# A gating unit that begins on an input whose norm is still being computed

## The reference, cut to what matters

```python
def rms_norm(x, g):
    y = x * lax.rsqrt(jnp.mean(x * x, axis=-1, keepdims=True) + EPS)
    return y * g

def adaln_input(h, mod, j, g):
    return rms_norm(h, g) * (1 + mod[:, :, 3 * j + 1]) + mod[:, :, 3 * j]

def sgu_mixer(xn, w_in, v_g, w_s, b_s, w_out):      # w_in: 1024 x 4096, w_out: 2048 x 1024
    u, v = jnp.split(jax.nn.gelu(xn @ w_in, approximate=False), 2, axis=-1)
    v = rms_norm(v, v_g)
    vg = v.reshape(B, nc, SGU_CHUNK, SGU_GROUPS, gw)          # chunks of 128 positions, 8 groups of 256
    sv = jnp.einsum('gts,bcsgd->bctgd', w_s, vg) + b_s.T[None, None, :, :, None]
    gated = u.reshape(B, nc, SGU_CHUNK, SGU_GROUPS, gw) * sv
    return gated.reshape(B, S, SGU_WIDTH) @ w_out

hp = hp + adaln_gate(m_ctx, 1) * sgu_mixer(adaln_input(hp, m_ctx, 1, norm_g[i, 1]), ...)
```

## Time and profile before

| | |
|---|---|
| median of 3 runs | 1591.44 us (1590.52 to 1593.1) |
| profiled execution, time | 1590.23 us |
| its span, first to last instruction | 1588.4 us |
| mean granted clock of PE | 0.989 |
| PE busy | 1541.1 us, 97% |
| DVE busy | 1106.8 us, 70% |
| ACT busy | 588.1 us, 37% |
| POOL busy | 71.5 us, 5% |
| down projection in front of the gating unit ends | 1078.0 us |
| gating unit's output projection begins | 1237.7 us |

### The profile page before, as it was taken

One profiled execution on the slowest core, in us unless ns is written; L12 is line 12 of the kernel. 1 busy time (PEld: TensorE's weight loads), 2 busy tenths in 40 slices (PEclk: granted clock), 3 DMA queues, 4 the chain that ended last, 5 costly groups with the idle time before them and its releaser, 6 DMA issues.

```text
span 1588.4 us, 23570 instructions
## 1 busy us (share of the span) xinstructions
PE 1541.1 (97%) x9183; PEld 1511.4 (95%) x9183; DVE 1106.8 (70%) x1501; ACT 588.1 (37%) x814; POOL 71.5 (5%) x55
## 2 busy tenths in 40 slices
PE   6999999989989999999999999998999999999999
PEld 6899999989749999999999999998999999999999
DVE  6868787867887877878878788776654355454423
ACT  3333332254474433332343333226434244333321
POOL 2000000023100100000020000001000010000000
PEclk9999999989999999999999999998999999999999
DMA  9255555635223354565635545563623432333332
GB/s 384 96 215 208 188 198 199 239 114 186 81 70 135 122 207 174 177 232 212 225 111 204 189 165 204 214 236 111 234 81 132 152 113 106 117 122 132 119 119 93
DMA packets 49648, 262.72 MB, mean 165 GB/s; under 512 B 6704, under 2 KB 7984, under 8 KB 27568
## 3 DMA queue, kind: packets, MB, share of 16 engines
q1 hardware_dynamic: 49584, 261.82, 45.2%
HBM read 259.57 MB, written 2.23 MB: 165 GB/s over the span
## 4 chain that ended last, share of the span: by engine, by line
PE 87%; DVE 5%; issue 3%; ACT 2%; DMA 2%; SPq 1%; POOL 1%; DVEq 0%; ACTq 0%; POOLq 0%
PE ps L1132 25%; PE ps L1131 25%; PE ps L1133 25%; PE ps L1165 3%; PE ps L1166 2%; PE ps L1168 2%; DVE mprod L746 1%; DMA raw_x<-panels 1%; ACT w_hi L506 1%; PE ps L1351 1%; PE ps L1434 1%; DVE x_lo L809 1%; DVE w_lo L738 1%; DMA raw<-panels 1%; PE ps L1211 0%
## 5 line engine op out<-in xcount | busy, mean ns | idle before, releaser
L506 ACT ACTIVATE w_hi<-raw 128x2048 fp32r<-128x2048 f32 x165 | 316.2, 1917 | 662.3 <-PE ps L1133 521.8
L1131 PE MATMUL ps<-x_hi,w_hi 128*128 128x386 f32 (+1 forms) x1536 | 524.4, 341 | 12.7 <-DVE x_lo L809 8.5
L738 DVE TENSOR_TENSOR w_lo<-raw,w_hi 128x2048 fp32r<-128x2048 f32 x163 | 373.2, 2290 | 233.0 <-ACT w_hi L506 231.9
L1132 PE MATMUL ps<-x_lo,w_hi 128*128 128x386 f32 (+1 forms) x1536 | 523.2, 341 | 0.0
L1133 PE MATMUL ps<-x_hi,w_lo 128*128 128x386 f32 (+1 forms) x1536 | 521.8, 340 | 0.0
L746 DVE SCALAR_TENSOR_TENSOR mprod<-mraw,cB 128x1024 f32<-128x1024 f32 x256 | 313.1, 1223 | 7.4
L1131 PEld LDWEIGHTS ps<-x_hi,w_hi 128*128 128x128 f32 x1536 | 290.6, 189 | 15.9 <-issue 6.7
L1132 PEld LDWEIGHTS ps<-x_lo,w_hi 128*128 128x128 f32 x1536 | 291.5, 190 | 0.5
L1133 PEld LDWEIGHTS ps<-x_hi,w_lo 128*128 128x128 f32 x1536 | 290.7, 189 | 0.0
L1133 PE MATMUL ps<-act_hi,w_lo 128*128 (+1 forms) x832 | 279.6, 336 | 0.0
L1131 PE MATMUL ps<-act_hi,w_hi 128*128 (+1 forms) x832 | 279.6, 336 | 0.0
(11 more groups left out here) (142 smaller groups left out, 1107.7 us busy)
## 6 DMA issues: line engine op xcount, KB each, us to landing
raw<-panels SPq DMA_DIRECT2D x165, 1024.0 KB, 5.0
mraw<-mod_rows SPq DMA_DIRECT2D x128, 512.0 KB, 3.5
mshift<-mod_rows SPq DMA_DIRECT2D x8, 512.0 KB, 15.8
raw_x<-panels SPq DMA_DIRECT2D x4, 1024.0 KB, 5.3
mscale<-mod_scale SPq DMA_DIRECT2D x6, 512.0 KB, 12.5
bias<-na_bias SPq DMA_DIRECT2D x1, 2048.0 KB, 8.2
h<-x_in_t SPq DMA_DIRECT2D x1, 1536.0 KB, 11.2
out<-h SPq DMA_DIRECT2D x4, 384.0 KB, 2.6
```

The source lines that it names most:

```text
L506: nc.scalar.activation(w_hi[q0 % 2][:, :], raw[q0 % 2][:, :], ACT.Copy).then_inc(hi_done, 1)
L738: nc.vector.tensor_tensor(w_lo[q0 % 2][:, :], raw[q0 % 2][:, :], w_hi[q0 % 2][:, :].bitcast(F32), ALU.subtract).then_inc(lo_done, 1)
L1131: mm(out, w[0][:, cols], xs[0], start=start, stop=False)
L1132: mm(out, w[0][:, cols], xs[1], start=False, stop=False)
```

## The change

The gating unit now begins with first_pair, like an FFN: panel G (U0, number Q_G = 109) and the spare panel (U1) on h * scale, then U2 (Q_U2 = 110) on the same x. While PE works on U2, ACT and DVE replace x in place, chunk by chunk, by the plain input that V needs, using four slots of sq. V0 follows, alone and chunk by chunk, then V1 to V7, U3, the mixing, and U4 to U7. The three early U panels are evicted with the factor to a new tile u_early and get their Gelu between V1 and V3. Their product with svb, rounding and subtraction are placed behind those of U3, U4 and U5 (U_TURNS). There is one more spare panel, loaded during the down projection before, and the panels behind it are numbered one lower.

```diff
+Q_G, Q_U2, Q_V, Q_U, Q_OUT1 = 109, 110, 111, 116, 124
+EARLY = (0, 1, 2)
+U_TURNS = (3, 0, 4, 1, 5, 2, 6, 7)
 # SP
+            def gate_behind_down():
+                sp.wait_ge(pe_done, down_panel(2))
+                spare_panel(3)
-            down(down_panel(2), GU, MOD_AT[2] + MOD_GU, MOD_DN[2])
+            down(down_panel(2), GU, MOD_AT[2] + MOD_GU, MOD_DN[2], gate_behind_down)
+            panel(Q_G, 0)
+            panel(Q_U2, 0)
...
-            for g in range(8):
+            for g in range(len(EARLY), 8):
                 panel(Q_U + g, 0)
 # POOL
-            norm(4, 4)
+            norm(4)
 # ACT
-            down(down_panel(2), GU)
-            squares(4)
+            down(down_panel(2), GU, lambda: split_spare(3))
+            scale_h(4, (NMOD + 3) * KD, 3)
+            split(Q_U2, 0)
+            split(Q_V, 0)
+            for k in range(KD):
+                base = (NMOD + 3) * KD
+                act.wait_ge(xv_scaled, k + 1)
+                for cond, cols in ((0, CTX), (1, LAT)):
+                    last = nc.scalar.activation(sq[:, k % 4, cols], sq[:, k % 4, cols], ACT.Identity,
+                                                bias=modT[:, base + k, cond:cond + 1], scale=aT[:, k, cond:cond + 1])
+                last.then_inc(xv_shifted, 1)
+                act.wait_ge(xv_shifted, k + 1)
+                if k < KD - 1:
+                    act.wait_ge(u2_done, k + 1)
+                else:
+                    act.wait_ge(pe_done, Q_U2 + 1)
+                nc.scalar.activation(x_hi[:, k, 0:T], sq[:, k % 4, :], ACT.Copy).then_inc(xvh_done, 1)
             split(Q_V + 1, 0)
-            make_x(4, (1, 1))
+            def early_gelu(g):
+                act.wait_ge(u_scaled, g + 1)
+                for a in range(2 * g, 2 * g + 2):
+                    for cond, cols in ((0, CTX), (1, LAT)):
+                        last = nc.scalar.activation(u_early[:, a, cols], u_early[:, a, cols], ACT.Gelu,
+                                                    bias=u_early[:, a, T + cond:T + cond + 1])
+                last.then_inc(silu_done, 1)
...
+                if 1 <= g <= len(EARLY):
+                    early_gelu(EARLY[g - 1])
-            for g in range(8):
-                done = UPAIR + g
-                act.wait_ge(pe_done, Q_U + g + 1)
-                act.wait_ge(actl_done, done)
-                bk = 2 * (g % 2)
-                nc.scalar.activation(tmp[:, 0:2, 0:T], ps[:, bk:bk + 2, 0:T], ACT.Gelu).then_inc(silu_done, 1)
-                split(Q_U + g + 2, 0)
+            for turn, g in enumerate(U_TURNS):
+                done = UPAIR + turn
+                at = 2 if g in EARLY else 0
+                if g not in EARLY:
+                    act.wait_ge(pe_done, Q_U + g + 1)
+                    act.wait_ge(actl_done, UPAIR + (U_TURNS.index(g - 1) + 1 if g - 1 not in EARLY else 0))
+                    bk = u_bank(g)
+                    nc.scalar.activation(tmp[:, 0:2, 0:T], ps[:, bk:bk + 2, 0:T], ACT.Gelu).then_inc(silu_done, 1)
+                    split(Q_U + g + 2, 0)
                 act.wait_ge(mul_done, done + 1)
-                nc.scalar.activation(act_hi[:, 2 * g:2 * g + 2, :], tmp[:, 0:2, 0:T], ACT.Copy).then_inc(acth_done, 1)
+                nc.scalar.activation(act_hi[:, 2 * g:2 * g + 2, :], tmp[:, at:at + 2, 0:T], ACT.Copy).then_inc(acth_done, 1)
 # DVE
-            down(down_panel(2), GU, 3, (1, 0), 0.5, MOD_AT[2] + MOD_GU, MOD_DN[2])
-            rms(4, Q_V + 1)
-            make_x(4)
+            down(down_panel(2), GU, 3, (1, 0), 0.5, MOD_AT[2] + MOD_GU, MOD_DN[2], spare=3)
+            split(Q_U2, 0)
+            factor(4)
+            def scale_t(k):
+                if k >= 4:
+                    dve.wait_ge(xv_done, k - 3)
+                nc.vector.tensor_tensor(sq[:, k % 4, :], h[:, k, :], sqsum[:, 0:T], ALU.mult).then_inc(xv_scaled, 1)
+            def low_v(k):
+                dve.wait_ge(xvh_done, k + 1)
+                nc.vector.tensor_tensor(x_lo[:, k, 0:T], sq[:, k % 4, :], x_hi[:, k, 0:T].bitcast(F32), ALU.subtract) \
+                    .then_inc(xv_done, 1)
+            def early_u(g, bank):
+                nc.vector.tensor_tensor(u_early[:, 2 * g:2 * g + 2, :], ps[:, bank:bank + 2, 0:XT],
+                                        sqsum[:, None, :].to_broadcast([P, 2, XT]), ALU.mult).then_inc(u_scaled, 1)
+            for k in range(4):
+                scale_t(k)
+            dve.wait_ge(pe_done, Q_G + 1)
+            early_u(0, gate_bank(0))
+            split(Q_V, 0)
+            for k in range(4):
+                low_v(k)
+                scale_t(k + 4)
+            dve.wait_ge(spare_pe, 4)
+            early_u(1, up_bank(0))
+            for k in range(4, KD):
+                low_v(k)
+            dve.wait_ge(pe_done, Q_U2 + 1)
+            early_u(2, 2)
+            split(Q_V + 1, 0)
+            dve.wait_ge(xv_done, KD)
...
+            for turn, g in enumerate(U_TURNS):
+                done = UPAIR + turn
+                at = 2 if g in EARLY else 0
+                if g not in EARLY:
+                    split(Q_U + g + 2, 0)
+                dve.wait_ge(silu_done, UPAIR + g + 1)
+                u = u_early[:, 2 * g:2 * g + 2, 0:T] if g in EARLY else tmp[:, 0:2, 0:T]
+                dve.wait_ge(actl_done, done)
+                nc.vector.tensor_tensor(tmp[:, at:at + 2, 0:T], u, svb[:, 2 * g:2 * g + 2, :], ALU.mult) \
+                    .then_inc(mul_done, 1)
                 dve.wait_ge(acth_done, done + 1)
...
 # PE
-            norm(4)
-            project_first(token_major, Q_V, QBANK, 4)
-            for g in range(2, 8):
-                pe.wait_ge(gelu_v, g - 1)
-                project(token_major, Q_V + g, 0, QBANK[g % 2])
+            first_pair(Q_G, 3, 4)
+            pe.wait_ge(lo_done, Q_U2 + 1)
+            for k in range(KD):
+                last = feature_major(Q_U2, 2, [(a, k) for a in range(2)], XT)
+                last.then_inc(u2_done if k < KD - 1 else pe_done, 1)
+            pe.wait_ge(lo_done, Q_V + 1)
+            pe.wait_ge(u_scaled, 1)
+            for k in range(KD):
+                pe.wait_ge(xv_done, k + 1)
+                last = token_major(Q_V, QBANK[1], [(t, k) for t in range(TT)])
+            last.then_inc(pe_done, 1)
+            pe.wait_ge(u_scaled, 3)
+            for g in range(1, 8):
+                if g > 1:
+                    pe.wait_ge(gelu_v, g - 1)
+                project(token_major, Q_V + g, 0, QBANK[(g + 1) % 2])
...
-            project(feature_major, Q_U, 0, 0)
+            project(feature_major, Q_U + 3, 0, u_bank(3))
...
-            for g in range(1, 8):
-                if g == 1:
-                    pe.wait_ge(sv_done, 10)
+            for g in range(4, 8):
+                if g < 6:
+                    pe.wait_ge(sv_done, 2 * g + 2)
...
-                project(feature_major, Q_U + g, 0, 2 * (g % 2))
+                project(feature_major, Q_U + g, 0, u_bank(g))
```

More of the change, by code:

```diff
@@ L42 @@
 XT = T + 2
-Q_F = (0, 45, 77, 133)
+Q_F = (0, 45, 77, 132)
+SPARE = (0, 1, 2, 4)
 Q_IN0, Q_OUT0 = 32, 41
-Q_V, Q_U, Q_OUT1 = 109, 117, 125
-Q_END = 165
+Q_G, Q_U2, Q_V, Q_U, Q_OUT1 = 109, 110, 111, 116, 124
+Q_END = 164
 MOD_GU = GU - 1
@@ L58 @@
 NORM_OF = (0, 2, 3, 5)
-ADDS = (0, 7, 10, 17, 24, 27)
-PLAIN = {1: 0, 4: 1}
-STAT_BANK = (7, 4, 7, 7, 4, 7)
+ADDS = (0, 7, 10, 17, 24, 31)
+STAT_BANK = (7, 4, 7, 7, 7, 7)
 def gate_panel(f, g):
@@ L81, in up_bank, with u_bank @@
     return 6 if g % 2 else 0
+def u_bank(g):
+    return 6 if g == len(EARLY) else 2 * (g % 2)
 def outs_until(block):
@@ L253, in build @@
         ol_done = sem("ol_done")
+        u_scaled = sem("u_scaled")
+        u2_done = sem("u2_done")
+        xv_scaled = sem("xv_scaled")
+        xv_shifted = sem("xv_shifted")
+        xvh_done = sem("xvh_done")
+        xv_done = sem("xv_done")
         ws_in = sem("ws_in")
@@ L700, in _ @@
                 for t in range(TT):
-                    last = nc.scalar.activation(v_tok[:, t, 256 * g:256 * g + 256], ps[:, QBANK[g % 2][t], 0:256], ACT.Gelu)
+                    last = nc.scalar.activation(v_tok[:, t, 256 * g:256 * g + 256], ps[:, QBANK[(g + 1) % 2][t], 0:256], ACT.Gelu)
                 last.then_inc(gelu_v, 1)
@@ L1110, in _ @@
             dve.wait_ge(sv_done, KS)
[L1111 to L1115, removed]
+            for turn, g in enumerate(U_TURNS):
[7 more added lines that the diff above has]
+                nc.vector.tensor_tensor(tmp[:, at:at + 2, 0:T], u, svb[:, 2 * g:2 * g + 2, :], ALU.mult) \
                     .then_inc(mul_done, 1)
                 dve.wait_ge(acth_done, done + 1)
-                nc.vector.tensor_tensor(act_lo[:, 2 * g:2 * g + 2, :], tmp[:, 0:2, 0:T],
+                nc.vector.tensor_tensor(act_lo[:, 2 * g:2 * g + 2, :], tmp[:, at:at + 2, 0:T],
                                         act_hi[:, 2 * g:2 * g + 2, :].bitcast(F32), ALU.subtract).then_inc(actl_done, 1)
-            down(Q_OUT1, KS // 2, 4, (1, 1), 1.0, spare=3)
```

(22 more changed lines are left out.)

22 lines of the change are left out of this document (11 added, 11 removed).

## The result

| | before | after |
|---|---|---|
| median | 1590.98 us (1589.53 to 1593.1, 4 runs) | 1580.62 us (1578.96 to 1584.25, 4 runs) |
| ratio | | 0.9939, 95% interval 0.9924 to 0.9955 |
| profiled execution, time and span | 1590.23 and 1588.4 us | 1584.25 and 1582.4 us |

The changed kernel is 10.4 us faster by the medians. The forecast was 9.2 us faster, 1582.2 us. The profiled executions differ by only 6.0 us, so the first thing to find out is where they part. I cut both at L, the last matmul of the second FFN's down projection, at the first matmul with act_hi, and at the next last matmul of a down projection.

What follows compares the result with a forecast made beforehand. TensorE, busy 97% of the span, was taken as the bound, with its waits and half-clock work the loss. -10.72 + 0.1 (Stall A) + 1.4 (Stall B) = -9.2 us, from 1591.44 to 1582.2; range 1580.2 to 1586.5.

Steps and rivals of the forecast that it cites:

- The old start's loss: From the last down matmul to V7's eviction: 81.08 us, less eight V panels' 67.92, so 13.16 us lost.
- The new start's loss: First_pair start, read at 797 us: 27.84 us for three panels against 25.47, so 2.37 us lost.
- Stall A: Handover of x during U2 and V0: PE waits for V1's split, 0.1 us, bounds 0 and 1.9.
- Stall B: U panels' tail: the output projection waits for U6's late act_lo, 1.4 us, bounds 0 and 2.4.
- At nothing: Early Gelus in ACT's idle time, the spare panel's load and split, and GpSimd's extra tiles: costed at zero.
- Rival 1: The clock falls at Stall B and costs 2.3 us: -6.9, 1584.5 us; chance 0.10.
- Rival 2: Handover of x later than timed, Stall A at 1.9: -7.4, 1584.0 us; chance 0.14.
- Rival 3: The U panels' tail fits after all, Stall B 0: -10.6, 1580.8 us; chance 0.08.
- Rival 4: Rewriting of x starts only after U2: 8.0 us delay plus 4.6 of clock, +3.4, 1594.8 us; chance 0.04.

Runs made afterwards that it cites:

- again: The changed kernel run once more, unedited, as yardstick for the first group: 1580.82 us, ratio 0.9935.
- again_2: The changed kernel unedited, run in the third group on another chip: 1582.57 us, ratio 0.9961.
- both_busy_start: Against both: 6 and 13 matmuls without use added in the two pauses of the program's first pair: 1579.31 us, ratio 0.9936.
- before_kept_busy: Kernel before, plus 12 and 17 unused 384-column matmuls behind the sums and the spread of norm 4: 1588.73 us, ratio 1.0.
- early_split: Changed kernel with only V1's split moved ahead of the last two chunks of x: 1580.1 us, ratio 0.9953.
- both: Changed kernel with late_wait's edit and V1's split ahead of the last two chunks of x: 1578.44 us, ratio 0.9925.
- late_wait: Changed kernel whose output projection waits for U6's act_lo only in its seventh panel: 1579.47 us, ratio 0.9925.
- pause_9: Changed kernel whose output projection's first matmul waits for U7's act_lo: 1591.6 us, ratio 1.0019.
- pause_2: Changed kernel whose output projection's first matmul also waits for U7's Gelu: 1585.37 us, ratio 0.9967.
- no_overlap: Changed kernel with DVE waiting for U2's end before its first product, so x is rewritten behind U2: 1588.61 us, ratio 0.9989.
- both_2: The kernel of both, unedited, run again in the third group: 1580.18 us, ratio 0.9945.

## Why the prediction was right, point by point

**The direction and the size.** The medians say -10.4 us beside the prediction, -10.1 with again and -6.2 with again_2; both stages together say -8.77 in the first profile and -8.72 in those of again and again_2. The forecast was -9.2, and the two stalls, 0.2 and 0.25 larger than forecast, make up the difference. What makes the medians wander lies mostly in unchanged code: runs of one kernel are 4 to 8 us apart (both_busy_start aside), and the profiles, in which the clock falls near 47 or 55 us or not, and again for a longer or shorter time near 100 and between 330 and 460, reach L between 1074.96 and 1080.76 us. 1582.2 against 1580.62 is off by 1.6 us: 0.5 by the base, 1591.44 against 1590.98, the rest by medians that differ by more than the stage does. So the stage carries the forecast, and the closeness of the median is partly luck: 1580.62 lies 0.4 us above the lower end of the range, and again_2 is only 6.2 us faster than its base.

**The old start's loss, 13.16.** It was read from the trace before, and before_kept_busy splits it: 2.1 clock, 11 chain.

**The new start's loss, 2.37.** One sign was forecast wrongly: U2 is evicted 32.53 behind L (L1145 at 1113.29), not 27.8, because the rewriting of x stands in front of it in DVE's queue. PE had finished it in time: V0 begins without a wait, 27.50 behind L. V7's eviction came 96.01 behind L (1176.77), forecast 95.86. In early_split, without stall A, it comes at 95.72, so the new start loses 2.33.

```profile
1108.09 0.34 PE L1211 MATMUL ps<-x_hi,w_lo 128*128 128x386 f32 x1
1108.26 0.28 PE L1243 MATMUL ps<-w_hi,x_hi 128*128 128x256 f32 x1
```

**Stall A, 0.1.** It is 0.31 (early_split, and both against late_wait). The chain was timed well: V1's split ended 36.14 behind L, where the forecast, spread 18.40 behind L plus 17.8, says 36.2. The error lies at its end. Without the stall (early_split) V1's first matmul comes 36.05 behind L, near the forecast's 36.1 (18.40 + 17.7). With it the matmul starts at 1117.05, 0.15 us behind the end of the split at 1116.90, and the sum has no such step.

**Stall B, 1.4.** It is 1.65 (late_wait). The mechanism was right in each step: a round of 9.45 forecast, 9.54 and 9.50 measured, twice, and the wait on act_lo named with its place. What was missing is 0.14 us in the two rounds and, again, 0.15 us from the end of the act_lo (1231.44) to the matmul that waited for it (1231.59).

**At nothing.** The Gelus of the early panels fit (V1 to V7 are evicted 8.49 us apart), and the output projection and all behind it kept their time within 0.1 us. The down projection that got the spare panel takes 91.35 us from its first matmul to its last in both profiles. ACT's load of Gelu's table (L740, at 1114.60 for 1.28 us) fell into its idle time before V0's end. The Trainium skill, "ScalarE: Activation LUTs", section "What ACT_TABLE_LOAD costs", gives 1283 ns for it; the trace agrees.

**Rival 1, the clock at stall B.** It didn't happen at 1.5 us. Longer pauses in its place, 2.40 and 9.25 us, did lower the clock, at 1.5 us each instead of my 2.3. The Trainium skill's rule, "TensorE: Matmul & The Clock Gate", section "HAM oscillation — how this bites in real kernels", that a waiting array is throttled and starts its next burst slowly, holds in these runs at 2.40, 5.75 and 9.25 us; it does not hold behind the pauses of 2.41 to 2.42 us at 53 us in six profiles (last section).

**Rival 2** had the right place and a sixth of the price. **Rival 3** (no stall B) is late_wait, not the changed kernel. **Rival 4** was mispriced: its delay is right (8.0, measured 7.9), its clock falls cost nothing. Even where true, the kernel would have been no slower than before (0.9979 to 1.0), so the forecast had no rival that ended on the other side. pause_9 shows what one would have needed: a pause of 9 us on PE's path.

## What to carry to other kernels

Count a stage as the time between two events of the bounding engine, take from the trace a start of the same form as the new one, and the gain follows as a difference of lost times. When an early result is finished later on in-order queues, ask for it as late as its consumer can: here two waits, moved, gave 2 us more. A clock fall and a wait behind it are not added: what the clock takes comes out of the next wait as long as that lasts.

## What the runs showed of the hardware that I had not expected

**The same pause cost the clock in some profiles and not in others, and the earlier fall was the free one.** Near 46 and 53 us PE waits twice for x_lo, in code that all 13 profiles share (both_busy_start fills most of the first pause and all of the second). The first pause varies from run to run, the second ends between 53.14 and 53.57 us in all of them:

| first pause, us | profiles | clock falls | second pause, us |
|---|---|---|---|
| 1.06 to 1.34 | before, again, late_wait, early_split, pause_9, before_kept_busy | no | 2.41 to 2.42 |
| 1.50 and 1.58 | after, pause_2 | behind the second, some 2.7 us lost by L | 2.42 and 2.43 |
| 1.81 to 2.15 | both, no_overlap, again_2, both_2 | behind the first, nothing lost at 53 us | 0.87 and 0.88 |

The table doesn't show that the first pause decides. Its length has a cause of its own: it ends between 46.21 and 46.64 us everywhere, and it is the longer the sooner PE's matmuls before it had come up to speed. Their distance falls from 0.32 to 0.18 us at 41.4 to 42.4 us in the first row, at 40.9 and 41.3 in the second, at 39.7 to 40.5 in the third. That moment sorts the profiles as well as the pause does, and no run parts the two.

The first pause in after, and in again_2 with the windows behind it:

```profile
46.46 0.44 PE L1209 MATMUL ps<-x_hi,w_hi 128*128 128x386 f32 x1 [1.50 <-DVE x_lo L852]
```
```profile
46.47 0.44 PE L1209 MATMUL ps<-x_hi,w_hi 128*128 128x386 f32 x1 [1.93 <-DVE x_lo L852]
```
```profile
46.00:48.00 2.00, 1.53 (x6) 1.53 (x7) 2.00 (x6) 0.61 (x2) 0.00 (x0) 0.76 0.00 0
48.00:50.00 2.00, 2.00 (x8) 2.00 (x7) 1.86 (x5) 0.00 (x0) 0.00 (x0) 0.50 0.00 0
```

In again_2 the slow matmuls only shorten the next wait, as in no_overlap; in after the fall comes behind the last wait and nothing takes it up. Why the same 2.4 us cost the clock at 1232 us, in pause_2, without another pause near, and not in the six profiles of the first row, stays open.

**Matmuls of 384 columns run at two paces at full clock.** In pause_2, both stages took 220.98 us where 217.35 + 0.9 of longer pause + 1.5 of clock make 219.8. The rest is not a wait. Behind the low clock the matmuls of the output projection start 0.1767 us apart on average (1236.81 to 1296.88, 340 intervals), in the changed kernel and in pause_9 0.1733, all at granted clock 1.00. Windows of 50 us, pause_2 and after (instructions in brackets):

```profile
1240.00:1290.00 50.00, 50.00 (x285) 50.00 (x285) 14.62 (x7) 13.31 (x7) 0.00 (x0) 1.00 0.36 135
```
```profile
1237.00:1287.00 50.00, 50.00 (x291) 50.00 (x290) 16.02 (x9) 14.15 (x8) 0.00 (x0) 1.00 0.40 147
```

Over the 384 matmuls of an output projection that is 1.3 us. The slower pace is no rarity: in the U panels, with as many columns, the matmuls start 0.1764 us apart in every profile (the 8.467 us of a U panel are 48 of them), and pause_2's output projection is the only one of the 65 down and output projections profiled that runs at it. What sets the pace is open; no run was made for it.
